# Weight columns stored in alternating pairs, one h_lo buffer, and activation buffers moved by 192 bytes in a ten-stage transformer kernel

## The reference

```python
x = x + 0.5 * g * swiglu(h, w_gate, w_up, w_down)      # D_FF = 2816, four times, layers 0 and 1 of block 1
y = mamba2_mixer(h, ...)        # layer 0 of block 1
y = moba_mixer(h, w_qkv, w_out) # layer 1 of block 1
mix = stick_breaking_attention(h, sb_w_in, sb_w_out)   # layer 0 of block 2
mix = dsa_attention(h, dsa_w_in, ...)                  # layer 1 of block 2
x = x + g2 * conv_ffn(h, w_up, conv_w, conv_b, w_down) # twice, block 2
```

## Time and profile before

| | before |
|---|---|
| median of 3 runs | 1782.38 us (1781.78 to 1782.6) |
| profiled execution's own time, which is its span | 1789.0 us |
| TensorE matmul busy | 1749.9 us, 98% of the span, 14686 records |
| TensorE weight load busy | 1700.5 us, 95% |
| VectorE busy | 1452.8 us, 81% |
| ScalarE busy | 956.5 us, 53% |
| data moved | 426.23 MB, mean 238 GB/s |
| TensorE clock granted | full in all of the 40 slices |

### The profile page before, as it was taken

How to read it: one execution, slowest core, us unless ns; L and a number is a source line. 1 busy time by engine, 2 the same in 40 slices (tenths; PEclk the granted TensorE clock), 3 DMA queues, 4 the chain that set the end, 5 groups by cost and what they waited for, 6 DMA issues and landing times.

```text
span 1789.0 us, 34260 instructions
## 1 busy us (share of the span) xinstructions
PE 1749.9 (98%) x14686; PEld 1700.5 (95%) x14686; DVE 1452.8 (81%) x1749; ACT 956.5 (53%) x1254; POOL 0.2 (0%) x4
## 2 busy tenths in 40 slices
PE   5999999999999999999999999999999999999999
PEld 4999999998999999999999999999999998989999
DVE  7799898888898889898557989765899887567766
ACT  4443466665533354445766444565655556775553
POOL 0000000000000000000000000000000000000000
PEclk9999999999999999999999999999999999999999
DMA  9998834344597949895444989343288545415551
GB/s 396 414 419 307 322 141 154 134 173 154 219 410 312 373 167 386 326 393 193 170 152 186 388 329 378 134 163 139 110 304 292 206 147 177 151 73 214 187 197 37
DMA packets 68149, 426.23 MB, mean 238 GB/s; under 512 B 7488, under 2 KB 10832, under 8 KB 31824
## 3 DMA queue, kind: packets, MB, share of 16 engines
q1 hardware_dynamic: 63936, 416.22, 60.5%
q10 hardware_dynamic: 4112, 8.62, 1.4%
HBM read 423.74 MB, written 3.17 MB: 239 GB/s over the span
## 4 chain that ended last, share of the span: by engine, by line
PE 90%; DVE 4%; ACT 3%; DMA 2%; issue 0%; DVEq 0%; SPq 0%; ACTq 0%
PE bank L1573 24%; PE bank L1574 24%; PE bank L1575 24%; PE bank L1630 2%; PE bank L1632 2%; PE bank L1631 2%; DMA raw<-weights 1%; PE bank L1686 1%; PE bank L1989 1%; DMA mix<-mods 1%; PE bank L1586 1%; PE bank L1600 1%; PE bank L1589 1%; PE bank L1822 1%; ACT w_hi L495 1%; DVE work L1034 1%
## 5 line engine op out<-in xcount | busy, mean ns | idle before, releaser
L1573 PE MATMUL bank<-h_hi,w_hi 128*128 128x256 f32 x2504 | 696.0, 278 | 0.0
L1574 PE MATMUL bank<-h_lo_rest,w_hi 128*128 128x256 f32 x2504 | 694.9, 278 | 0.0
L1575 PE MATMUL bank<-h_hi,w_lo 128*128 128x256 f32 x2504 | 694.8, 277 | 0.0
L913 DVE TENSOR_TENSOR w_lo<-raw,w_hi 128x2048 fp32r<-128x2048 f32 x267 | 609.5, 2284 | 90.4 <-ACT w_hi L495 89.3
L495 ACT ACTIVATE w_hi<-raw 128x2048 fp32r<-128x2048 f32 x276 | 527.9, 1913 | 160.0 <-PE bank L1575 145.7
L1573 PEld LDWEIGHTS bank<-h_hi,w_hi 128*128 128x128 f32 x2504 | 472.8, 189 | 0.0
L1574 PEld LDWEIGHTS bank<-h_lo_rest,w_hi 128*128 128x128 f32 x2504 | 470.2, 188 | 0.0
L1575 PEld LDWEIGHTS bank<-h_hi,w_lo 128*128 128x128 f32 x2504 | 470.1, 188 | 0.0
L1573 PE MATMUL bank<-a_hi,w_hi 128*128 128x256 f32 x1280 | 358.5, 280 | 1.2 <-DVE a_lo L1291 0.8
L1575 PE MATMUL bank<-a_hi,w_lo 128*128 128x256 f32 x1280 | 355.3, 278 | 0.0
L1574 PE MATMUL bank<-a_lo,w_hi 128*128 128x256 f32 x1280 | 355.3, 278 | 0.0
(11 more groups left out here) (303 smaller groups left out, 1989.4 us busy)
## 6 DMA issues: line engine op xcount, KB each, us to landing
raw<-weights SPq DMA_DIRECT2D x276, 1024.0 KB, 5.4
modws<-mods SPq DMA_DIRECT2D x144, 768.0 KB, 6.6
mix<-mods SPq DMA_DIRECT2D x5, 1024.0 KB, 8.8
mix<-mods ACTq DMA_DIRECT2D x8, 512.0 KB, 13.3
biases<-scratch ACTq DMA_DIRECT2D x1, 2048.0 KB, 13.1
mix<-biases ACTq DMA_DIRECT2D x4, 512.0 KB, 4.0
modws<-mods SPq DMA_DIRECT2D x1, 1024.0 KB, 11.7
x<-xin SPq DMA_DIRECT2D x1, 1024.0 KB, 10.9
```

The lines of the kernel that those rows point to most:

```text
L913: eng.tensor_tensor(w_lo[g % NW][:, :], raw[g % NRAW][:, :], w_hi[g % NW][:, :], ALU.subtract).then_inc(sems["wlo"], 1)
L1573: eng.matmul(dst, ah, bh, start=start, stop=False, skip_group_check=skip)
L1574: eng.matmul(dst, ah, bl, start=False, stop=False, skip_group_check=skip)
L1575: return eng.matmul(dst, al, bh, start=False, stop=stop, skip_group_check=skip)
```

## The change

The diff does four things.

1. On the host, `wide` and `deep` store the 256 columns of each pair of 128-column groups alternately: column 0 of the first group, column 0 of the second, column 1 of the first, and so on. TensorE then loads 128 weights per partition at a step of 2 elements (8 bytes), over 1,024 bytes where it was 512. The second group starts 4 bytes after the first. For the v projection, `moving` keeps the old layout. The blocks have the same bytes in number, and ScalarE and VectorE convert them as before.
2. `h_lo_rest` and `h_lo_first` become one buffer `h_lo_all` of 8 slices.
3. `gap` buffers are moved so that `h_hi`, `h_lo_all`, `a_hi`, `a_lo` and `mix` start at remainder 0 of 256, where the weight slots stay at 128. `work` stays at 64.
4. The special order for kk = 0 goes: every kk calls `three`.

The filler matmuls use the step of 2 for the stationary side, and their moving side is the same slot as before.

```diff
         gs = sb("gs", [P, NJOB, 8])
+        gap = sb("gap", [P, 48])
         h_hi = sb("h_hi", [P, KT, T], F32R)
-        h_lo_rest = sb("h_lo_rest", [P, KT - 1, T], F32R)
-        gap = sb("gap", [P, 16])
-        h_lo_first = sb("h_lo_first", [P, T], F32R)
-        gap2 = sb("gap2", [P, 48])
+        h_lo_all = sb("h_lo_all", [P, KT, T], F32R)
+        gap2 = sb("gap2", [P, 16])
...
-            return h_lo_rest[:, kk - 1, :] if kk else h_lo_first[:, :]
+            return h_lo_all[:, kk, :]
...
         acg = sb("acg", [64, 384], F32R)[:, :]
+        gap3 = sb("gap3", [P, 48])
         a_hi = sb("a_hi", [P, 2, T], F32R)
...
-                hi, lo = [w.rearrange("p (k n) -> p k n", k=KT) for w in begin(st, i, a, b)]
-                both = [(m, slice(m * P, (m + 1) * P), dst[:, m * T:(m + 1) * T]) for m in range(2)]
+                hi, lo = [w.rearrange("p (k n) -> p k n", k=KT) if tokens else
+                          w.rearrange("p (k c m) -> p k m c", k=KT, m=2) for w in begin(st, i, a, b)]
+                both = [(m, slice(m * P, (m + 1) * P) if tokens else m, dst[:, m * T:(m + 1) * T]) for m in range(2)]
...
-                            if tokens and kk == 0:
-                                eng.matmul(d, h_lo(kk)[:, part], hi[:, kk, :], start=True, stop=False)
-                                eng.matmul(d, h_hi[:, kk, part], hi[:, kk, :], start=False, stop=False)
-                                eng.matmul(d, h_hi[:, kk, part], lo[:, kk, :], start=False, stop=False)
-                            elif tokens:
+                            if tokens:
                                 mm = three(d, h_hi[:, kk, part], h_lo(kk)[:, part], hi[:, kk, :], lo[:, kk, :],
                                            kk == 0, kk == KT - 1)
-                            elif kk == 0:
-                                eng.matmul(d, hi[:, kk, part], h_lo(kk), start=True, stop=False)
-                                eng.matmul(d, hi[:, kk, part], h_hi[:, kk, :], start=False, stop=False)
-                                eng.matmul(d, lo[:, kk, part], h_hi[:, kk, :], start=False, stop=False)
                             else:
-                                mm = three(d, hi[:, kk, part], lo[:, kk, part], h_hi[:, kk, :], h_lo(kk),
+                                mm = three(d, hi[:, kk, part, :], lo[:, kk, part, :], h_hi[:, kk, :], h_lo(kk),
                                            kk == 0, kk == KT - 1)
...
-                hi, lo = [w.rearrange("p (k n) -> p k n", k=2) for w in begin(st, i, a, b)]
+                hi, lo = [w.rearrange("p (k j c m) -> p k j m c", k=2, j=4, m=2) for w in begin(st, i, a, b)]
...
-                        mm = three(acc(m), hi[:, kk, part], lo[:, kk, part], a_hi[:, kk, :], a_lo[:, kk, :],
+                        mm = three(acc(m), hi[:, kk, m // 2, m % 2, :], lo[:, kk, m // 2, m % 2, :], a_hi[:, kk, :], a_lo[:, kk, :],
...
     def wide(w):
         n = w.shape[1] // 256
+        return w.reshape(KT, P, n, 2, P).transpose(2, 1, 0, 4, 3).reshape(n, P, 2048)
+
+    def moving(w):
+        n = w.shape[1] // 256
         return w.reshape(KT, P, n, 256).transpose(2, 1, 0, 3).reshape(n, P, 2048)
 
     def deep(w):
         n = w.shape[0] // 256
-        return w.reshape(n, 2, P, D).transpose(0, 2, 1, 3).reshape(n, P, 2048)
+        return w.reshape(n, 2, P, 4, 2, P).transpose(0, 2, 1, 3, 5, 4).reshape(n, P, 2048)
```

More of the change, by code:

```diff
@@ L1585, in gemm @@
                         for m, part, d in both:
-                            eng.matmul(d, hi[:, kk, part], h_hi[:, kk, :], start=kk == m == 0, stop=False,
+                            eng.matmul(d, hi[:, kk, part, :], h_hi[:, kk, :], start=kk == m == 0, stop=False,
                                        skip_group_check=True)
                             if st:
-                                eng.matmul(d, lo[:, kk, part], h_hi[:, kk, :], start=False, stop=False,
+                                eng.matmul(d, lo[:, kk, part, :], h_hi[:, kk, :], start=False, stop=False,
                                            skip_group_check=True)
@@ L1599, in gemm @@
                         for m, part, d in both:
-                            mm = eng.matmul(d, hi[:, kk, part], h_lo(kk), start=False, stop=kk == KT - 1,
+                            mm = eng.matmul(d, hi[:, kk, part, :], h_lo(kk), start=False, stop=kk == KT - 1,
                                             skip_group_check=True)
@@ L1605, in gemm @@
                         for m, part, d in both:
-                            eng.matmul(d, hi[:, kk, part], h_lo(kk), start=kk == m == 0, stop=False,
+                            eng.matmul(d, hi[:, kk, part, :], h_lo(kk), start=kk == m == 0, stop=False,
                                        skip_group_check=True)
-                            eng.matmul(d, hi[:, kk, part], h_hi[:, kk, :], start=False, stop=False,
+                            eng.matmul(d, hi[:, kk, part, :], h_hi[:, kk, :], start=False, stop=False,
                                        skip_group_check=True)
@@ L1612, in gemm @@
                         for m, part, d in both:
-                            mm = eng.matmul(d, lo[:, kk, part], h_hi[:, kk, :], start=False, stop=kk == KT - 1,
+                            mm = eng.matmul(d, lo[:, kk, part, :], h_hi[:, kk, :], start=False, stop=kk == KT - 1,
                                             skip_group_check=True)
@@ L1643, in gemm_out @@
                     for m in range(KT):
-                        part = slice(m * P, (m + 1) * P)
-                        mm = three(acc(m), hi[:, kk, part], lo[:, kk, part], a_hi[:, kk, :], a_lo[:, kk, :],
+                        mm = three(acc(m), hi[:, kk, m // 2, m % 2, :], lo[:, kk, m // 2, m % 2, :], a_hi[:, kk, :], a_lo[:, kk, :],
                                    fresh and kk == m % 2 == 0, False, True)
@@ L1690, in fill @@
             def fill(st):
-                hi = begin(st, 0, 0, 0)[0].rearrange("p (k n) -> p k n", k=KT)
+                hi = begin(st, 0, 0, 0)[0]
+                turned_hi = hi.rearrange("p (k c m) -> p k m c", k=KT, m=2)
                 for n in range(FILL.get(st, 14)):
-                    eng.matmul(bank[5][:, 0:T], hi[:, n % KT, 0:P], hi[:, n % KT, :], start=True, stop=True)
+                    at = n % KT * T
+                    eng.matmul(bank[5][:, 0:T], turned_hi[:, n % KT, 0, :], hi[:, at:at + T], start=True, stop=True)
             def norm(st):
@@ L1762, in last @@
                     for n in range(14):
-                        eng.matmul(bank[5][:, 0:T], hi[:, 0, 0:P], hi[:, 0, 0:T], start=True, stop=True)
+                        eng.matmul(bank[5][:, 0:T], hi[:, 0, 0, 0, :], w_hi[(k.block(st) + NBLK[stages[st]] - 1) % NW][:, 0:T],
+                                   start=True, stop=True)
                 ready()
@@ L1768, in last @@
                         squares(st + 1, 0)
-                    part = slice(m * P, (m + 1) * P)
                     for kk in range(1 if m < early else 0, 2):
-                        mm = three(acc(m), hi[:, kk, part], lo[:, kk, part], ahi[:, kk, :], alo[:, kk, :],
+                        mm = three(acc(m), hi[:, kk, m // 2, m % 2, :], lo[:, kk, m // 2, m % 2, :], ahi[:, kk, :], alo[:, kk, :],
                                    False, False, True)
@@ L2158, in attn @@
     def attn(w, wo):
-        pipelined([wide(w[:, :D]), wide(w[:, D:2 * D]), wide(w[:, 2 * D:])], deep(wo))
+        pipelined([wide(w[:, :D]), wide(w[:, D:2 * D]), moving(w[:, 2 * D:])], deep(wo))
     def mamba():
```

9 lines of the change are left out of this document (4 added, 5 removed).

## The result

| | before | changed |
|---|---|---|
| median | 1782.41 us | 1859.55 us (1858.62 to 1862.45, 4 runs) |
| ratio | | 1.0421, 95% interval 1.0399 to 1.0442 |
| profiled execution's span | 1789.0 us | 1860.7 us |

The account below looks back on a forecast made before the run. TensorE's dense matmul pace, 113.3 to 120 ns, was taken to bound the kernel. Falling to 110 ns, feed-forward windows, other stages (16) and stage ends (3) summed to 61 us, 3.4%: 1721 us, range 1700 to 1800.

Parts of the forecast that it names:

- I take 110 ns: Pace assumed for every dense TensorE matmul after the change, between bounds of 106.7 and 120 ns; read off transposes.
- rival D: Weight loads at a step of 2 open twice as many lines and set TensorE's pace: slower, 1844 us; chance 0.22.
- D's price of 62 us: All stages' dense matmuls at 120 ns, the worst pace of a row, giving 1844 us.
- The distance of 128 bytes: Load and moving side both read 1,024 bytes, staying about 128 apart by remainder, so the pace loss goes.
- Rows 8: Profile rows in dsa: matmuls with 8-column weights at 117 ns, cited against the loss being between the two streams.
- The special kk = 0: Its matmuls, three times 344 at about 120 ns; undoing it alone worth 2.5 us or nothing.
- The sum's base: Matmul counts times (pace minus 110 ns), using profiled stage paces; 61 us, 3.4% of the 1789.0 us span, scaled to the median.
- B: Rival: only the slow pace goes and 113.3 ns becomes the pace everywhere; 22 us less, 1760 us; chance 0.26.
- D's second price: 117.6 ns everywhere, both column groups like the slow stages: about 5,400 x 3.5 + 3,792 x 2.3 = 28 us, 1810 us.
- host layout, conversions and DMA: Same bytes, rows and instructions as before, so costed at 0, hidden or not.
- The v projection: 384 matmuls at 117.9 ns, weights still contiguous, activations moved to 0; -1.8 to +0.8 us, taken as 0.
- The cap that VectorE was to put on stage 0: Stage 0, 70 to 215 us: VectorE becomes the bound, so half of the 10.0 us gain was taken, 5.

Follow-up runs that it names:

- contig_64: The changed kernel with weight columns contiguous again and activations back at remainder 64, still one h_lo buffer and no special kk = 0; 1804.85 us, ratio 1.0107.
- contig_0: The changed kernel with weight columns contiguous again, activations still at remainder 0; 1834.20 us, ratio 1.0281.
- reset_ffn: contig_64 with two float32r matmuls of 16 columns added ahead of each feed-forward stage's third block; 1778.81 us, ratio 0.9992 against the kernel before.
- sweep3: Separate kernel of matmul bursts alone, varying weight step, moving columns and short matmuls ahead; with 16 moving columns, 118.0 ns at a step of 2.

## Why the prediction was wrong, step by step

**What bounds the kernel** was right: the pace of TensorE's dense stretches made all of the 77 us but 4.

**The step that failed** is "I take 110 ns, the lowest pace a row shows for pairs of a load and a matmul", and with it the picture it came from, that two reading places that keep 128 bytes apart lose nothing. Measured: 121.2 ns in the burst and 120.9 in the kernel. Three things were wrong in it.

- *The load was not free.* I had it at up to 111 ns from a row with contiguous weights, and assumed that time for a step of 2. At a step of 2 it is 118 ns against 16 moving columns, above the 113.3 of the matmul, and 233 at a step of 4. That alone closed the gain: against 256 columns no remainder that was tried gives a step of 2 less than 119.0. This is rival D's mechanism, and its 0.22 was too little, since it needed only 2 ns of loss in the load to decide, as I had written. D's price of 62 us at 120 ns was near the 77 measured in part by luck: the 120 came from a row with contiguous weights, and of the 77 us the first two of the three steps, 22 and 29, come without the pairs (contig_64, contig_0).
- *The distance of 128 bytes is not the best one.* With contiguous weights it costs 118.7 ns against 113.3 at 64 below, 29 us in the kernel (contig_0 against contig_64), though five of contig_64's six feed-forward stages had the slower pace; against reset_ffn it is 55 us.
- *The floor is not 110.* That row was of transposes in float32. For float32r with 256 moving columns no stretch here ran below 113.3, not with 8 weight columns either. Rows 8 were the warning, and the warning was half right: their 117 ns come with weights whose remainder changes from one matmul to the next; at remainder 128 the same narrow loads run at 113.3.

**The special kk = 0** I put down as a cost of 2.5 us or nothing. Without it and its slice, with all else as before, the kernel takes 22 us more (contig_64). What goes with them is that most stages have the fast pace: four of six in the profile before, one of six in contig_64. By itself the special order saves nothing: reset_ffn, which has no special order and has the fast pace by other means, takes no more than the kernel before. Whether the order or the slice does it no run tells apart, and how stays open.

**The sum's base.** "A whole stage keeps one pace" was not so for stage 0, which changed at 72.5 us. I built the sum on paces of an execution in which two of six feed-forward stages were slow, and scaled it by 3.4% to the median, which most likely has none. A rival at 113.3 ns everywhere (B, 22 us) could have won little more than 10 in the typical run. D's second price, at 117.6 ns, counts 5,400 matmuls at the fast pace where its four windows hold 6,037: it should be 30 us and not 28.

**Costed at nothing and rightly so:** host layout, conversions and DMA. VectorE's 1455.9 and ScalarE's 956.3 us are within 4 us of before. The v projection is unchanged in kind: 118.5 ns on the mean now, against 117.8, some 0.3 us for 384 matmuls. The cap that VectorE was to put on stage 0 never came to bear.

**The rules of the Trainium skill.** The Trainium skill, SBUF — State Buffer, "Door 1: The DMA port swizzle", asks for at least two hits in a 16-byte line for full bandwidth. The loads agree in kind and not in the edge: two hits in a line (a step of 2) take 118 ns where four take at most 112, and one hit 233. Its rule in "Who interferes with whom", that TensorE's two read ports are independent and never wait, doesn't describe the paces of 113.3 to 123.3 ns by remainder alone.

**What stays open:** what meets in the 4 to 9 ns that the distance decides, why 64 bytes below is good and 60 is not, and by what rule a short matmul or a pause changes the phase: one that was put in did so each time, three lost the fast pace where two kept it, and two gave it in all but a few places. No other picture of what the two streams share was tested here.

## What to carry to other kernels

When one instruction sets the time, read its pace from start to start in several stages before reasoning about its operands: two paces for one shape mean that something other than addresses is at work, and that one profile is one draw. Keep the stationary side contiguous for matmuls of 256 moving columns in 32 bits; an access that was hidden with a few ns to spare must be priced in its new form by a row or by a burst of its own. A burst of 48 matmuls per layout in a small kernel priced three corners of the full one to within 0.3 ns, in one run; the fourth, at the good distance, it had 3 ns too low, since a burst has one phase and a kernel draws one per stage. And read the granted clock of every stretch of such a sweep before its pace.

## What the runs showed of the hardware

- A load of 128 float32r weights at a granted clock of 1.00: at most 112 ns contiguous, 118 ns at a step of 2 elements, 233 ns at a step of 4 (sweep3). At 0.50 pairs of a load and a matmul ran at 213 ns at a step of 2, and still at 233 at a step of 4.
- float32r, 128 x 128 against 256 columns at the 2.4 GHz level: 113.3 ns at best, with the moving side's address 64 bytes below the weights' by remainder of 256; 116.7 to 120.0 at the other steps of 32 bytes, 118.6 and 122.2 at 4 bytes to either side of the best, 123.3 at 12 bytes below it.
- At that best distance a dense stretch runs at 113.3 or at 117.8 ns, by what stands just ahead of it, and mostly keeps it, over 1,400 matmuls and more; one short matmul put in changed it 24 times of 24, and a pause of TensorE did so once in the kernel before. The other engines' and queues' traffic changed none of the 20 pairs of bursts in which it ran throughout.
- Two short float32r matmuls of 16 columns put ahead of a stretch gave the fast pace in 12 stages of 12, in one trace each of two kernels (four of them had it without, in the kernel before). In bursts two float32r ones gave it 12 times of 12 in each of two series, but not always in bursts with another order of matmuls, another slice or short matmuls put in.
